# One down chunk of each small expert as a plain F32 product straight from the ring of weights

## The reference, cut to what matters

```python
hidden = silu(x_e @ w_gate[e]) * (x_e @ w_up[e])      # x_e: the tokens of expert e
y_e = hidden @ w_down[e]                              # (tokens of e) x 1024
out[token] += gate_weight[token, e] * y_e
```

## Time and profile before

| | |
|---|---|
| median of 3 runs | 1894.48 us (1893.77 to 1898.86) |
| span of the profiled execution | 1894.2 us |
| TensorE busy | 1833.4 us, 97% |
| TensorE weight loads busy | 1524.4 us, 80% |
| VectorE busy | 1469.6 us, 78% |
| ScalarE busy | 1213.1 us, 64% |
| GpSimd busy | 142.4 us, 8% |
| DMA | 511.54 MB, mean 270 GB/s |
| chain that ended last | PE 71%, DVE 17%, DMA 6%, ACT 3%, issue 2% |

### The profile page before, as it was taken

How to read it: one execution, slowest core, us unless ns; L and a number is a source line. 1 busy time by engine, 2 the same in 40 slices (tenths; PEclk the granted TensorE clock), 3 DMA queues, 4 the chain that set the end, 5 groups by cost and what they waited for, 6 DMA issues and landing times.

```text
span 1894.2 us, 22429 instructions
## 1 busy us (share of the span) xinstructions
PE 1833.4 (97%) x9190; PEld 1524.4 (80%) x9190; DVE 1469.6 (78%) x1418; ACT 1213.1 (64%) x1258; POOL 142.4 (8%) x118
## 2 busy tenths in 40 slices
PE   7999999999999999999999999999999999999997
PEld 6888878888988788888788887878888787888875
DVE  5646565444579764458879899999989999998997
ACT  6555555433564454345637788988778898777784
POOL 2511100000100140004130000000000000000000
PEclk9999999999999999999989999999999999999999
DMA  8533345544442465344358999999999999999994
GB/s 296 177 134 134 134 154 204 198 178 151 170 169 89 156 224 198 134 160 154 131 202 342 373 354 423 420 422 420 395 363 362 419 420 422 418 379 368 370 420 167
DMA packets 154782, 511.54 MB, mean 270 GB/s; under 512 B 4431, under 2 KB 8898, under 8 KB 140338
## 3 DMA queue, kind: packets, MB, share of 16 engines
q1 hardware_dynamic: 152674, 504.53, 69.2%
q0 software_dynamic: 1392, 4.53, 0.7%
q10 hardware_dynamic: 608, 0.99, 0.1%
HBM read 508.98 MB, written 1.05 MB: 269 GB/s over the span
## 4 chain that ended last, share of the span: by engine, by line
PE 71%; DVE 17%; DMA 6%; ACT 3%; issue 2%; POOL 0%; ACTq 0%; SPq 0%; DVEq 0%; POOLq 0%
PE PS L442 19%; PE PS L444 19%; PE PS L443 19%; DVE WLX L1911 6%; DVE WLB L1911 6%; DMA ring<-in_moe_w_down 4%; PE PS L900 2%; PE PS L1139 1%; PE PS L1140 1%; ACT WHX L1290 1%; DMA ring<-in_moe_w_gate 1%; PE PS L1070 1%; PE PS L1072 1%; ACT WHB L1290 1%; PE PS L596 1%
## 5 line engine op out<-in xcount | busy, mean ns | idle before, releaser
L1911 DVE TENSOR_TENSOR WLB<-ring,WHB 128x2048 fp32r<-128x2048 f32 (+1 forms) x344 | 636.6, 1867 | 113.2 <-ACT WHB L1290 112.7
L1290 ACT ACTIVATE WHB<-ring 128x2048 fp32r<-128x2048 f32 (+1 forms) x344 | 531.5, 1557 | 300.1 <-PE PS L444 270.6
L1911 DVE TENSOR_TENSOR WLX<-ring,WHX 128x2048 fp32r<-128x2048 f32 (+1 forms) x216 | 469.1, 2192 | 51.2 <-ACT WHX L1290 51.0
L1290 ACT ACTIVATE WHX<-ring 128x2048 fp32r<-128x2048 f32 (+1 forms) x216 | 392.6, 1834 | 156.4 <-PE PS L444 124.8
L442 PE MATMUL PS<-WHB,XH 128*128 128x512 f32 (+1 forms) x640 | 255.2, 399 | 8.6 <-DVE XL L1945 2.4
L444 PE MATMUL PS<-WHB,XL 128*128 128x512 f32 (+1 forms) x640 | 247.7, 387 | 0.0
L443 PE MATMUL PS<-WLB,XH 128*128 128x512 f32 (+1 forms) x640 | 247.1, 386 | 0.0
L442 PEld LDWEIGHTS PS<-WHB,XH 128*128 128x128 f32 x640 | 121.1, 189 | 36.7 <-issue 6.2
L2831 POOL TENSOR_TENSOR SM<-SM,MH 128x8 f32<-128x8 f32 (+3 forms) x28 | 38.1, 1366 | 1392.1 <-DVE SM L1924 1392.1
L444 PEld LDWEIGHTS PS<-WHB,XL 128*128 128x128 f32 x640 | 120.8, 189 | 25.0
L443 PEld LDWEIGHTS PS<-WLB,XH 128*128 128x128 f32 x640 | 121.3, 190 | 21.8
(11 more groups left out here) (422 smaller groups left out, 3407.6 us busy)
## 6 DMA issues: line engine op xcount, KB each, us to landing
ring<-in_moe_w_gate SPq DMA_DIRECT2D x56, 2048.0 KB, 11.1
ring<-in_moe_w_up SPq DMA_DIRECT2D x56, 2048.0 KB, 10.9
ring<-in_moe_w_down SPq DMA_DIRECT2D x56, 2048.0 KB, 11.7
ring<-in_w_in SPq DMA_DIRECT2D x13, 2048.0 KB, 7.8
ring<-in_hg_w_in SPq DMA_DIRECT2D x8, 2048.0 KB, 8.4
ring<-in_da_w_in SPq DMA_DIRECT2D x6, 2048.0 KB, 7.9
ring<-in_w_gate SPq DMA_DIRECT2D x5, 2048.0 KB, 7.5
ring<-in_w_up SPq DMA_DIRECT2D x5, 2048.0 KB, 7.6
```

Source lines behind the costliest of these rows:

```text
L1290: e.activation(hi, src, ACT.Copy).then_inc(s_hi, 1)
L1911: e.tensor_tensor(lo, src, hi.bitcast(F32), ALU.subtract).then_inc(s_lo, 1)
```

## The change

One chunk of each small expert (chunk 3 of experts 1, 2, 4, 5, chunk 2 of expert 7) is `WHOLE`. Its two pieces are left out of the list of pieces, so that neither ScalarE nor VectorE splits them. VectorE multiplies Silu and up straight into the first 64 columns of each block of a new buffer SGW, whose other columns GpSimd has set to zero; hi and lo parts of these rows are not made. TensorE multiplies SGW by the four rows of blocks of the ring's slot in plain F32, 8 products of 128x512. The next load of this slot waits for that product (s_whole) instead of s_lo. SGW lies over the small tables NG, GM and LAMB. The places at which the pieces of the other chunks are split keep their count, so they hold the pieces that come next in the list.

```diff
--- before.py
+++ after.py
@@ -33,6 +33,7 @@
 RANK = (0, 3, 4, 1, 5, 6, 2, 7)
 LIGHT = (1, 2, 4, 5, 7)
 HEAVY = NE - len(LIGHT)
+WHOLE = {1: 3, 2: 3, 4: 3, 5: 3, 7: 2}
 
 
 def steps_of(ex):
@@ -144,9 +145,9 @@
         IDB = sb("IDB", [128, 128], BF16)
         CSB = sb("CSB", [128, 128], BF16)
         BC = sb("BC", [128, 2, D])
-        NG = sb("NG", [128, 128])
-        GM = sb("GM", [128, 2, 64])
-        LAMB = sb("LAMB", [128, 256])
+        SGW = sb("SGW", [128, 512])
+        NG, LAMB = SGW[:, 0:128], SGW[:, 256:512]
+        GM = SGW[:, 128:256].rearrange("p (a n) -> p a n", a=2)
         BFG = sb("BFG", [128, 8])
         WFG = sb("WFG", [128, 8, 8])
         WRT = sb("WRT", [128, 8, 8])
@@ -209,6 +210,7 @@
         s_tab, s_x, s_vec, s_bc, s_ln, s_outd, s_lvt, s_pset = (sem(n) for n in ("s_tab", "s_x", "s_vec", "s_bc", "s_ln", "s_outd", "s_lvt", "s_pset"))
         s_tab2, s_kz, s_kd = sem("s_tab2"), sem("s_kz"), sem("s_kd")
         s_hid, s_hth, s_htl, s_sgt, s_ub, s_perm = sem("s_hid"), sem("s_hth"), sem("s_htl"), sem("s_sgt"), sem("s_ub"), sem("s_perm")
+        s_sgw, s_whole = sem("s_sgw"), sem("s_whole")
         s_nb, s_hp, s_hd = sem("s_nb"), sem("s_hp"), sem("s_hd")
         s_lbd, s_lbe, s_sg, s_kk, s_lf, s_cc, s_q0, s_set = (sem(n) for n in ("s_lbd", "s_lbe", "s_sg", "s_kk", "s_lf", "s_cc", "s_q0", "s_set"))
         s_ed, s_ee, s_qs, s_ks, s_lv, s_stt, s_vv = (sem(n) for n in ("s_ed", "s_ee", "s_qs", "s_ks", "s_lv", "s_stt", "s_vv"))
@@ -291,13 +293,17 @@
 
 
         PIECES, PLACE, AFTER, LAST_OF = [], [], [], []
-        FIRST = {}
+        FIRST, DIRECT = {}, {}
         lay = {}
         for part_name, part_list, n_p in (("A", WL_A, 4), ("F1", WL_F1, 2), ("C", WL_C, 4), ("F2", WL_F2, 2), ("E", WL_E, 4), ("M", WL_M, 2)):
             FIRST[part_name] = len(PIECES)
             for item in part_list:
+                kind, _, ex = item[0].partition(" ")
+                whole = kind == "down" and WHOLE.get(int(ex)) == item[1] // 4
+                if whole:
+                    DIRECT[int(ex)] = len(LAST_OF)
                 step = -(-item[3] // n_p)
-                for j in range(n_p):
+                for j in range(0 if whole else n_p):
                     k = len(PIECES)
                     m = k - FIRST[part_name]
                     if n_p == 4:
@@ -1121,7 +1127,24 @@
                         t = e.transpose(PS[6][:, 128 * j:128 * j + 128], inner(HID[:, i, :], j), ident)
                 t.then_inc(banks.put(("mt", ex, c), 6, out=(s_htl, 24 + n + 1)), 1)
 
+            def whole_down(ex, c):
+
+                k = sorted(WHOLE).index(ex)
+                i = DIRECT[ex]
+                pe.wait_ge(s_sgw, 1)
+                pe.wait_ge(s_htl, 24 + NCH * ex + c + 1)
+                pe.wait_ge(s_ring[SLOT[i]], 16 * (USE[i] + 1))
+                for j in range(4):
+                    for q in range(2):
+                        at_ = 1024 * j + 512 * q
+                        t = e.matmul(PS[4 + q][:, :], SGW[:, 128 * j:128 * j + 128], slot(i)[:, at_:at_ + 512], start=False, stop=False)
+                t.then_inc(s_whole, 1)
+                T["whole", k] = (s_whole, k + 1)
+
             def expert_down(ex, c):
+                if WHOLE.get(ex) == c:
+                    whole_down(ex, c)
+                    return
                 i = (NCH * ex + c) % 2
                 for h2 in range(2):
                     hi, lo, used = next_piece(f"down {ex}", 4 * c)
@@ -1781,11 +1804,12 @@
                     if T["light at", n]:
                         a.wait_ge(s_htl, 24 + T["light at", n])
                     e.activation(SGT[:, :], PS[6][:, 0:256], ACT.Silu).then_inc(s_sgt, 1)
-                if stage == 1 or not light:
+                if (stage == 1 or not light) and WHOLE.get(ex) != c:
                     if n >= 2:
-                        a.wait_ge(*T["ht read", (n - 2) // NCH, (n - 2) % NCH, "m"])
+                        m = n - 4 if WHOLE.get((n - 2) // NCH) == (n - 2) % NCH else n - 2
+                        a.wait_ge(*T["ht read", m // NCH, m % NCH, "m"])
                     if light:
-                        a.wait_ge(s_ub, T["light", n] + 1)
+                        a.wait_ge(s_ub, T["split", n] + 1)
                         h = HTH[:, n % 2, :].rearrange("p (j x n) -> p j x n", j=4, x=2)[:, :, 0, :]
                         e.activation(h, SGT[:, :].rearrange("p (j n) -> p j n", j=4), ACT.Copy).then_inc(s_hth, 1)
                     elif stage == 0:
@@ -1801,11 +1825,14 @@
                     e.activation(ZH[:, 512 * q:512 * q + 512], PS[4 + q], ACT.Copy, scale=GS[ex]).then_inc(s_zh, 1)
 
 
-            k, at_ = 0, 0
+            k, k2, k3, at_ = 0, 0, 0, 0
             for n in range(NCH * NE):
+                whole = WHOLE.get(n // NCH) == n % NCH
+                T["turned", n] = k3
+                k3 += not whole
                 if n // NCH in LIGHT:
-                    T["light", n], T["light at", n] = k, at_
-                    k, at_ = k + 1, n + 1
+                    T["light", n], T["light at", n], T["split", n] = k, at_, k2
+                    k, k2, at_ = k + 1, k2 + (not whole), n + 1
             for q in range(2):
                 gathered(0, q)
             a.wait_ge(s_rt, 1)
@@ -1855,8 +1882,9 @@
 
                     if more:
                         gathered(ex + 1, 0)
-                    for i in range(len(before)):
-                        pieces_done(2)
+                    for i, (x, c) in enumerate(before):
+                        if WHOLE.get(x) != c:
+                            pieces_done(2)
                         if more and i == 0:
                             gathered(ex + 1, 1)
                         if ex == NE - 1 and s == 3 and i == 0:
@@ -2609,16 +2637,26 @@
 
             def expert_turned(ex, c, stage):
                 n = NCH * ex + c
-                if ex in LIGHT:
+                if WHOLE.get(ex) == c:
+                    if stage == 0:
+                        v.wait_ge(s_sgt, T["light", n] + 1)
+                        v.wait_ge(s_sgw, 1)
+                        k = sorted(WHOLE).index(ex)
+                        if k:
+                            v.wait_ge(*T["whole", k - 1])
+                        h = SGW[:, :].rearrange("p (j x n) -> p j x n", j=4, x=2)[:, :, 0, :]
+                        up, g = (x.rearrange("p (j n) -> p j n", j=4) for x in (PS[6][:, 256:512], SGT[:, :]))
+                        e.tensor_tensor(h, up, g, ALU.mult).then_inc(s_htl, 1)
+                elif ex in LIGHT:
                     if stage == 0:
                         v.wait_ge(s_sgt, T["light", n] + 1)
                         e.tensor_tensor(SGT[:, :], PS[6][:, 256:512], SGT[:, :], ALU.mult).then_inc(s_ub, 1)
                     else:
-                        v.wait_ge(s_hth, 24 + n + 1)
+                        v.wait_ge(s_hth, 24 + T["turned", n] + 1)
                         h = HTH[:, n % 2, :].rearrange("p (j x n) -> p j x n", j=4, x=2)
                         e.tensor_tensor(h[:, :, 1, :], SGT[:, :].rearrange("p (j n) -> p j n", j=4), h[:, :, 0, :].bitcast(F32), ALU.subtract).then_inc(s_htl, 1)
                 elif stage == 0:
-                    v.wait_ge(s_hth, 24 + n + 1)
+                    v.wait_ge(s_hth, 24 + T["turned", n] + 1)
                     e.tensor_tensor(HTL[:, n % 2, :], PS[6], HTH[:, n % 2, :].bitcast(F32), ALU.subtract).then_inc(s_htl, 1)
 
             def expert_up(ex, c):
@@ -2963,6 +3002,8 @@
             gain_rows(2, 1, 0)
             p.wait_ge(s_hh, 1)
             e.tensor_tensor(HL[:, 0, :], H[:, 0, :], HH[:, 0, :].bitcast(F32), ALU.subtract).then_inc(s_hl, 1)
+            p.wait_ge(s_doo, 4)
+            e.memset(SGW[:, :], 0.0).then_inc(s_sgw, 1)
             p.wait_ge(s_hp, 11)
             p.wait_ge(s_hd, 1)
             norm_vectors(3)
@@ -2992,7 +3033,9 @@
 
             def load(i):
                 t, n = WL[i][3:]
-                if BEFORE[i] >= 0:
+                if BEFORE[i] in DIRECT.values():
+                    q.wait_ge(*T["whole", list(DIRECT.values()).index(BEFORE[i])])
+                elif BEFORE[i] >= 0:
                     q.wait_ge(s_lo, LAST_OF[BEFORE[i]] + 1)
                 elif SLOT[i] == NSLOT:
                     q.wait_ge(s_used, FIRST["E"])
```

## The result

| | before | after |
|---|---|---|
| median | 1894.78 us (4 runs) | 1942.33 us (4 runs, 1939.65 to 1945.02) |
| span of the profiled execution | 1894.2 us | 1937.9 us |
| TensorE, VectorE, ScalarE busy | 1833.4, 1469.6, 1213.1 us | 1860.2, 1446.1, 1194.3 us |
| DMA, mean | 270 GB/s | 264 GB/s |

The account below looks back on a forecast made before the run. DMA transfer was taken to bound the small experts, TensorE the large. Delays of 2 x 7.3 (experts 1, 4), 2 x 8.1 (2, 5) and 1 (7) sum to 31.8 us, giving 1926 us; 8-in-10 range 1902 to 1938.

Parts of the forecast that it names:

- The first: Small experts: VectorE is the bound, loads run faster when slots come sooner, no delays arise; 1882 us, chance 8%.
- the fourth rival: Whole chunks: the saved 5 us of VectorE work pay for the delay; 1894 to 1898 us, chance 4%.
- the second: Whole chunks: the order costs nothing, only the held slot and longer product count; 1906 us, chance 18%.
- the third: SP's three loads issued together share the DMA engines, the first landing some 5 us later or more; 1936 to 1946 us, 8%.
- It takes 1.8 us (1193.68 to 1195.46 before), so the whole product runs from 1200.5 to 1207.4: Expert 1, TensorE after the late gating: the gather takes 1.8 us, then the whole product 6.9 us.
- the surcharge of 3.1 us: TensorE, each whole chunk: the plain F32 product takes 6.9 us against the old chunk's 3.76, 3.1 us more.
- worked off again: Expert 1: TensorE starts the next expert 8.2 us late and works that off to the DMA's 7.3.
- The order's delay: Before the next expert's gather: chunk 4's gating stands behind down 4's split, so the gather starts 5.0 us late.
- In a stage that the DMA bounds: Small experts: DMA transfer is last, so saved splits count nothing and a load 7.3 us late is never regained.
- the load behind the held slot: Ring slot, released only after the whole product: without the order's delay, the next load lands 2.2 us late.
- a lone load: Ring load issued to an idle DMA: lands 7.6 us after issue; the skill's formula gives 6.8 us.
- upper rival: SP's three loads issued at once share DMA engines, the first landing some 5 us later; 1936 to 1946 us, 8%.

Follow-up runs that it names:

- experiment 8: Changed kernel with SP also waiting for the landing of the load held by the whole product before issuing the next: 1952.44 us.
- experiment 2: Changed kernel with twelve extra plain F32 products keeping TensorE busy ahead of the gather of experts 2, 3, 5 and 6: 1929.98 us.
- experiment 7: Kernel before with down 3 and down 4's first piece split ahead of chunk 4's gating: 1935.94 us; second edit, later count restored, 1927.09 us.
- experiment 5: Changed kernel with empty places kept for the whole chunk's pieces and only half of the whole product's records done: 1890.29 us against 1894.12.
- experiment 6: Kernel before with seven extra plain F32 products behind the first down chunk of the last step of experts 1, 2, 4 and 5: 1907.37 us.
- experiment 1: Changed kernel with the whole chunk's two pieces kept as empty places in both splitting engines' counts: 1903.81 us against 1894.12.
- experiment 3: Changed kernel with chunk 1 instead of chunk 3 taken whole in experts 1, 2, 4 and 5: 1903.59 us against 1894.12.
- experiment 4: Changed kernel with empty places kept and chunk 1 instead of chunk 3 taken whole in experts 1, 2, 4 and 5: 1905.16 us against 1895.23.
- experiment 9: Changed kernel, look-ahead unchanged, with chunk 4's gating put ahead of the split of down 4 on both engines: 1908.93 us against 1894.39.

## Why the prediction was right or wrong, point by point

- **The mechanism and its places were right.** ScalarE's place now holds a load that lands 5 us later, the gating queues behind it, the gather waits for bank 6, the slot is released late and the DMA runs dry, in experts 1, 2, 4 and 5 and not in 7 (0.6 us by the table, 1 expected). The first and the fourth rival are refuted by the result, the second by the 5.07 us of idle TensorE, the third by experiment 8.
- **The step that failed** is "It takes 1.8 us (1193.68 to 1195.46 before), so the whole product runs from 1200.5 to 1207.4", and with it the surcharge of 3.1 us in the sum. Both durations were taken at a clock of 1.00, and put behind an idle stretch that the forecast had itself put there. Measured are 3.4 us for each gather, and for the products up to 9.2, against 6.9 forecast and 6.5 with the clock up. The four places term by term, from the traces (each term against the trace before, us):

| | experts 1, 2, 4, 5 | sum | forecast |
|---|---|---|---|
| gather starts late (the order) | 4.1, 5.5, 3.9, 5.7 | 19.2 | 20.0 |
| gather takes longer | 1.6, 1.6, 1.6, 1.6 | 6.5 | 0 |
| whole product | 8.0, 8.0, 9.2, 8.5 | 33.7 | 27.6 |
| less the old chunk | 3.8, 3.7, 3.8, 5.3 | 16.6 | 15.0 |
| worked off again | none | 0 | 1.6 |

The two slow terms are 6.5 and 6.1 us, 12.6 together, and experiment 2 gave back 12. That is as much as the whole gap by the profiled spans (43.7 against 31.8), and most of the 15.7 us by the medians.
- **The order's delay was right at the gather and too low in its price.** It was bounded at 5.0 us; the gathers start 3.9 to 5.7 us late. But alone, with three pieces ahead of the gating in place of one, it costs 8.4 us at each place (experiment 7), mostly because the clock falls with it.
- **"In a stage that the DMA bounds" was half right.** The saved splits are indeed worth little (at most 3.8 us of up to 25, experiment 5). But TensorE's time was to be worked off in the small experts at a slack of 6.4 us in 160, and experiment 6 charges it in full: 13.7 us for 11.4 (one slow stretch of the clock, in expert 4, is among the 13.7). The four gathers are points at which ScalarE waits for TensorE and the next splits for ScalarE, and there TensorE's lateness becomes the DMA's.
- **Terms that were right:** the surcharge of the plain F32 product with the clock up, 3.1 us forecast and 2.8 measured (6.55 less 3.76); the load behind the held slot, 2.2 us late in the second rival's working and 2.0 measured in experiment 1; and that rival's sum, 12 us for the change without the order's delay, where experiment 1 measured 9.7.
- **Small slips that move nothing:** a lone load was put at 7.6 us from one row, where the page of the kernel before has 7.5 to 8.4 for the five kinds of loads in earlier stages, and experiment 8 has 7.6 to 9.1. At 6.8 us for it the sum would have been 1.6 us smaller and not 3, since only experts 1 and 4 use it; the Trainium skill (DMA: Bandwidth & Descriptors, Anatomy of one DMA) has fitted these figures to transfers that GpSimd issues, while the loads here are SP's. 35 chunks at 14.9 us are 522 us, not 515.
- The range ended at 1938, for its upper rival had TensorE's clock constant too.

## What to carry to other kernels

Where engines name their work by place and not by item, leaving items out moves a wait onto whatever stands behind the place: list what is queued behind each place and who waits for it, and keep empty places or move the urgent work ahead. Where a forecast puts an idle stretch of several us on TensorE, price the work behind it at the lower clock as well: here 5 us of waiting cost another 3 us each time (12.6 / 4). That an engine's work is hidden by a full DMA says nothing of an engine beside it whose lateness reaches the loads through a shared buffer.

## What the runs showed of the hardware that was not expected

The granted clock also fell where TensorE had hardly been idle. The kernel before has such a place itself, at the gather ahead of expert 6, where down 3 took 5.3 us in place of 3.8:

```profile
1629.34 1.08 PE L1072 MATMUL PS<-PO,XH 128*128 128x128 f32 x8 [1.23 <-DVE HTH L2619]
...
1632.00:1634.00 2.00, 2.00 (x6) 1.57 (x5) 2.00 (x2) 1.09 (x3) 0.00 (x0) 0.50 1.05 410
```

In experiment 6 it fell around the gather at the end of expert 4, with a wait of 0.49 us ahead of it (0.61 from 1534 to 1536):

```profile
1530.00:1532.00 2.00, 2.00 (x18) 1.91 (x18) 2.00 (x2) 2.00 (x3) 0.00 (x0) 1.00 1.05 409
1532.00:1534.00 2.00, 2.00 (x7) 1.56 (x6) 2.00 (x2) 0.99 (x3) 0.00 (x0) 0.54 1.06 408
```

In experiment 2 it stood at 0.50 at 1204 to 1206, under the plain F32 product, after a wait of 0.83 us; experiments 3 and 4 have three more such places, after waits of 1.00, 0.89 and 1.70 us. All lie at or just behind a gather that had waited. In experiments 1, 5 and 9, the first halves of the twelve gathers at these places don't wait, and the clock stays at 1.00 at all of them. But a wait alone doesn't do it: the kernel before has waits of 0.96, 1.00 and 0.99 us at its other three gathers and keeps 1.00. No run was made to tell what decides it.
